# Attention scores copied to SBUF by the maximum pass, and one softmax scaling moved to the output copy

## What is computed

```python
def diff_core(q, k, v, lam):                       # "differential": 4 heads, two maps each
    s = einsum('bqhid,bkhid->bhiqk', q, k) * (DA ** -0.5)
    p = softmax(s, axis=-1)
    w = p[:, :, 0] - lam * p[:, :, 1]
    return einsum('bhqk,bkhd->bqhd', w, v)

def mla_core(qn, qr, kn, kr, v):                   # "latent": 8 heads
    s = (einsum('bqhd,bkhd->bhqk', qn, kn) + einsum('bqhd,bkd->bhqk', qr, kr)) * MLA_SCALE
    return einsum('bhqk,bkhd->bqhd', softmax(s, axis=-1), v)
```

## Time and profile before

| | us |
|---|---|
| median of 3 runs (4333.61 to 4336.67) | 4334.28 |
| the profiled execution | 4333.03 |
| its span in the trace | 4330.8 |
| PE busy | 3899.8 (90%) |
| VectorE busy | 2267.4 (52%) |
| ScalarE busy | 1575.8 (36%) |
| maxima L1061, x160 | 128.7 |
| exponentials from PSUM, 128x768, x128 | 113.8 |

### The profile page before, as it was taken

One profiled execution on the slowest core, in us unless ns is written; L12 is line 12 of the kernel. 1 busy time (PEld: TensorE's weight loads), 2 busy tenths in 40 slices (PEclk: granted clock), 3 DMA queues, 4 the chain that ended last, 5 costly groups with the idle time before them and its releaser, 6 DMA issues. The chain is left out here.

```text
span 4330.8 us, 53542 instructions
## 1 busy us (share of the span) xinstructions
PE 3899.8 (90%) x19922; PEld 3032.5 (70%) x19922; DVE 2267.4 (52%) x3759; ACT 1575.8 (36%) x2699; POOL 317.8 (7%) x282
## 2 busy tenths in 40 slices
PE   4987888999899898988899899979879998988998
PEld 3865556777788787865666588857568886657886
DVE  6345476854554475355632455354655535565552
ACT  2234463112443354234531344234444424343431
POOL 0000001111000000010000100002110010401001
PEclk8999999999999999999999999989889999989999
DMA  5100003552233244210012233322123322202332
GB/s 170 59 27 11 8 1 133 189 188 97 78 97 102 91 156 137 68 32 18 1 52 87 80 92 96 99 68 69 44 59 97 101 98 80 83 15 78 97 100 79
DMA packets 86727, 350.82 MB, mean 81 GB/s; under 512 B 9520, under 2 KB 9648, under 8 KB 85680
## 3 DMA queue, kind: packets, MB, share of 16 engines
q1 hardware_dynamic: 72752, 298.53, 21.9%
q0 software_dynamic: 13824, 50.34, 3.5%
HBM read 346.73 MB, written 2.10 MB: 81 GB/s over the span
## 5 line engine op out<-in xcount | busy, mean ns | idle before, releaser
L492 DVE TENSOR_TENSOR split_low<-weight_ring,split_high 128x1024 fp32r<-128x1024 f32 (+1 forms) x456 | 606.3, 1330 | 892.3 <-ACT split_high L484 877.5
L484 ACT ACTIVATE split_high<-weight_ring 128x1024 fp32r<-128x1024 f32 (+1 forms) x474 | 524.7, 1109 | 1043.6 <-PE banks L1364 470.0
L1492 PE MATMUL banks<-normed_high,split_high 128*128 128x512 f32 (+1 forms) x1760 | 654.0, 372 | 78.1 <-DVE normed_low L431 37.9
L1492 PE MATMUL banks<-normed_low,split_high 128*128 128x512 f32 (+1 forms) x1760 | 650.9, 370 | 0.0
L1492 PE MATMUL banks<-normed_high,split_low 128*128 128x512 f32 (+1 forms) x1760 | 650.6, 370 | 0.0
L1492 PEld LDWEIGHTS banks<-normed_high,split_high 128*128 128x128 f32 x1760 | 334.5, 190 | 141.2 <-issue 85.4
L1492 PEld LDWEIGHTS banks<-normed_low,split_high 128*128 128x128 f32 x1760 | 334.8, 190 | 55.0
L1492 PEld LDWEIGHTS banks<-normed_high,split_low 128*128 128x128 f32 x1760 | 334.3, 190 | 55.7
L1364 PE MATMUL banks<-hidden_high,split_high 128*128 128x512 f32 (+1 forms) x880 | 324.3, 369 | 8.0 <-DVE split_low L492 8.0
L1364 PE MATMUL banks<-hidden_low,split_high 128*128 128x512 f32 (+1 forms) x880 | 323.7, 368 | 0.0
L1364 PE MATMUL banks<-hidden_high,split_low 128*128 128x512 f32 (+1 forms) x880 | 323.7, 368 | 0.0
(11 more groups left out here) (286 smaller groups left out, 6757.7 us busy)
## 6 DMA issues: line engine op xcount, KB each, us to landing
weight_ring<-in_up SPq DMA_DIRECT2D x220, 512.0 KB, 3.6
weight_ring<-in_down SPq DMA_DIRECT2D x80, 704.0 KB, 4.0
modulation_ring<-in_ada POOLq DMA_DIRECT2D x80, 512.0 KB, 4.8
weight_ring<-in_merge SPq DMA_DIRECT2D x48, 768.0 KB, 4.5
weight_ring<-in_inputs SPq DMA_DIRECT2D x36, 512.0 KB, 3.6
weight_ring<-in_out SPq DMA_DIRECT2D x32, 512.0 KB, 3.6
latents<-in_ada POOLq DMA_DIRECT2D x16, 512.0 KB, 4.7
weight_ring<-in_xbc SPq DMA_DIRECT2D x16, 512.0 KB, 3.6
```

What stands on the lines that cost most here:

```text
L484: act.activation(k.splits[0][:, (n0 + panel) % RING, 0:width], k.slot(n0 + panel)[:, 0:width], ACT.Copy).then_inc(k.high_ready.sem, 1)
L492: dve.tensor_tensor(k.splits[1][:, s, 0:width], k.ring[:, s, 0:width], k.splits[0][:, s, 0:width].bitcast(F32), ALU.subtract).then_inc(k.l ...
L1492: last = pe.matmul(sums(r, half), w, x, start=(c + j == 0), stop=(c == KT - 1 and j == 2))
```

## The change

A column of zeros is written once. Differential and latent steps get it as their mask, repeated over all keys, so that they take the branches for masked steps: the maximum pass adds zero and writes the scores to `probs`, the exponential works there in place, and `scores_free` gives the maximum's semaphore. In differential steps map 0 isn't scaled any more: map 1's inverse is multiplied by map 0's sum besides -lambda, and the store multiplies the 128x128 output with map 0's inverse. Each reciprocal of such a step from t = 2 on also waits for the store before it. The parameter `adjacent`, true in all calls, goes away; the loops are those it had chosen.

```diff
@@ prepare @@
             dve.memset(k.head_squares[:, :], 1.0)
+            dve.memset(k.scalars[:, 14:15], 0.0)
...
@@ attention, VectorE, normalise @@
+                if combined and t >= 2:
+                    dve.wait_ge(*k.output_stored(t - 1))
                 link(dve.reciprocal(inverse, total))
                 if combined and j == 1:
-                    link(dve.tensor_tensor(inverse, inverse, step["subtract"], ALU.mult))
+                    link(dve.scalar_tensor_tensor(inverse, inverse, one(sums, m - 1), step["subtract"], ALU.mult,
+                                                  ALU.mult))
                     first = k.probs[:, (m - 1) % 4, 0:step["keys"]]
                     dve.scalar_tensor_tensor(first, p, inverse, first, ALU.mult, ALU.add).then_inc(
                         k.probs_ready.sem, 1)
                 elif combined:
-                    link(dve.tensor_scalar(p, p, inverse, None, ALU.mult))
+                    pass
...
@@ attention, VectorE, store @@
                     dve.wait_ge(*k.output_ready(t + 1))
-                    dve.tensor_copy(steps[t]["out"], result(t)).then_inc(k.output_stored.sem, 1)
+                    if combined:
+                        copied = dve.tensor_scalar(steps[t]["out"], result(t), one(inverses, 2 * t), None, ALU.mult)
+                    else:
+                        copied = dve.tensor_copy(steps[t]["out"], result(t))
+                    copied.then_inc(k.output_stored.sem, 1)
...
@@ mix_branches, differential @@
             steps.append(step(maps, end, [[values[:, c, P * h:P * h + P] for c in range(end // P)]],
-                              mixed[:, h, at:at + P], subtract=k.scalars[:, 8 + l:9 + l],
+                              mixed[:, h, at:at + P], mask=k.scalars[:, 14:15].to_broadcast([P, end]),
+                              subtract=k.scalars[:, 8 + l:9 + l],
                               square=squares[:, 6 * h + at // P:6 * h + at // P + 1]))
...
@@ mix_branches, latent @@
             steps.append(step(maps, end, [[values[:, c, 128 * pair + 64 * j:128 * pair + 64 * j + 64]
                                            for c in range(end // P)] for j in range(2)],
-                              mixed[:, 4 + pair, at:at + P]))
+                              mixed[:, 4 + pair, at:at + P], mask=k.scalars[:, 14:15].to_broadcast([P, end])))
```

More of the change, by code:

```diff
@@ L951, in project_latents, with attention @@
            constants_loaded=16)
-def attention(k, steps, turned, adjacent=False, scratch=None):
+def attention(k, steps, turned, scratch=None):
     nc = k.nc
@@ L988, in _, with score @@
         def _(pe):
-            def score(t, maps):
-                for j in maps:
+            def score(t):
+                for j in range(2):
                     if t >= 1:
@@ L1027, in _ @@
                 if t < U:
-                    score(t, (0, 1) if adjacent else (0,))
-                if not adjacent and t >= 2:
-                    weigh(t - 2)
+                    score(t)
                 if 1 <= t <= U:
                     turn(t - 1, 0)
-                if adjacent and t >= 2:
+                if t >= 2:
                     weigh(t - 2)
-                if not adjacent and t < U:
-                    score(t, (1,))
                 if 1 <= t <= U and per == 2:
@@ L1097, in _ @@
                     normalise(t - 1, 0)
-                    if adjacent:
-                        normalise(t - 1, 1)
+                    normalise(t - 1, 1)
                 if t < U:
                     maximum(t, 0)
[L1102 to L1105, removed]
+                    maximum(t, 1)
                 if t >= 2:
                     store(t - 2)
-                if t < U and not adjacent:
-                    maximum(t, 1)
             k.linked = linked
@@ L1144, in _ @@
             for t in range(U + 1):
-                if adjacent and 1 <= t:
+                if t >= 1:
                     copy(t - 1, 0)
@@ L1148, in _ @@
                     exponential(t, 0)
[L1149 to L1152, removed]
+                    exponential(t, 1)
                 if t >= 1 and per == 2:
                     copy(t - 1, 1)
-                if t < U:
-                    if not adjacent:
-                        exponential(t, 1)
                 if scratch is not None and t >= 3:
@@ L1671, in mix_branches @@
             steps.append(step(maps, end, [[values[:, c, P * h:P * h + P] for c in range(end // P)]],
-                              mixed[:, h, at:at + P], subtract=k.scalars[:, 8 + l:9 + l],
+                              mixed[:, h, at:at + P], mask=k.scalars[:, 14:15].to_broadcast([P, end]),
+                              subtract=k.scalars[:, 8 + l:9 + l],
                               square=squares[:, 6 * h + at // P:6 * h + at // P + 1]))
-    attention(k, steps, turned, adjacent=True, scratch=rope_queries.rearrange("p a b -> p (a b)").rearrange("p (a b) -> p a b", b=P))
+    attention(k, steps, turned, scratch=rope_queries.rearrange("p a b -> p (a b)").rearrange("p (a b) -> p a b", b=P))
     project_latents(k, l, context, mixed, keys, values, latents, rope_queries, squares)
@@ L1687, in mix_branches @@
                                            for c in range(end // P)] for j in range(2)],
-                              mixed[:, 4 + pair, at:at + P]))
-    attention(k, steps, turned, adjacent=True)
+                              mixed[:, 4 + pair, at:at + P], mask=k.scalars[:, 14:15].to_broadcast([P, end])))
+    attention(k, steps, turned)
     steps, wide = [], k.tables[:, 0:5 * P]
@@ L2198, in second_branches @@
                                   mask=k.table("wide")[:, BANK - end:BANK], gate=gate[1 + j], first=False, last=(j == 1)))
-    attention(k, steps, [tile[:, 24 + s, :] for s in range(4)], adjacent=True)
+    attention(k, steps, [tile[:, 24 + s, :] for s in range(4)])
 def plain_norm(k, gain, target, split=None, summed=True, ahead=0, block=None):
```

## The result

The changed kernel takes 4298.57 us (median of 4 runs, 4292.65 to 4299.79) against 4333.94 us before (4 runs, 4333.07 to 4336.67): ratio 0.9915, interval 0.9904 to 0.9927. A second set on another chip gave 4301.54 us (5 runs, 4293.32 to 4303.37) against 4330.53 (15 runs): 0.9932, interval 0.9919 to 0.9946. The forecast was 4312.5 us with a range from 4303 to 4322, a ratio of 0.995. The direction was right, and the gain was 35 us (29 in the second set) where 21.8 had been worked out.

The account below looks back on a forecast made before the run. TensorE nearly bounds latent steps; a loop of exponentials, combination, turn and copy bounds differential ones. Gains less losses made 21.7 us off the profiled 4333.0, plus 1.25 to reach the median's scale: 4312.5 us, range 4303 to 4322.

Parts of the forecast that it names:

- Latent, steady steps: Latent attention, 768-key steps: score released by the maximum, 6.61 to about 6.05 us, 24 x 0.56 = 13.4 us gained.
- Latent, from 256 to 768 keys: Latent attention, three steps reaching 768 keys from 256: TensorE goes earlier, 3 x 0.96 = 2.9 us gained.
- Stage starts: First scores of the stages start sooner: 1.8 and 1.2 us gained in latent attention, 2.7 in both differential stages.
- Differential attention, low clock: Layer 0's differential stage: three low-clock steps each shorten by 0.76 us through the early score, 2.3 us gained.
- 256-key steps: Differential attention, 8 steps of 256 keys: scaling no longer behind VectorE's late store, 0.2 us each, 1.6 us gained.
- Rival A: Layer 0's differential stage: the clock stays up, 4 to 8 us more gained, 4306 us; chance 0.13.
- Losses in the differential loop: Differential attention, 40 steps: exponentials from SBUF lose 2.2 us, the reciprocals' extra wait 2.0 us.
- added wait: Differential loop: reciprocals also wait for the store, 0.05 us a step, 40 x 0.05 = 2.0 us lost.
- C: Copying maximum becomes the bound: at 1.9 us a pass, differential loses 42 us, latent 7, 4383 us; chance 0.03.
- B: Latent attention: 24 steps become TensorE-bound and the clock nods to 0.95, gain 14 us, 4320 us; chance 0.12.
- D: Differential loss is larger, 8 us instead of 4.2, and the low clock gives nothing back: 4319 us; chance 0.05.
- Exponentials from SBUF by the page: Differential exponentials: the skill's page gives 43 ns more each, the rows 26; loss 3.4 us instead of 2.2.

Follow-up runs that it names:

- start kernels: Changed kernel with the first three steps of each differential and latent stage released late, 4308.05 us; with only those steps released early, 4326.68 us.
- differential attention alone: Changed kernel with latent attention put back as before, so only differential attention is changed: 4321.05 us against 4329.86, ratio 0.9979.
- filler kernel: Kernel before, with TensorE carrying out the weighing of each 256-key differential step three times, no wait changed: 4325.66 us against 4329.73, ratio 0.9992.

## Why the prediction missed

- **Latent, steady steps: right.** 6.61 to 6.05 us, from the sum of PE's parts. So were the price of the exponential (927 ns for 924) and the cover of the maxima.
- **Latent, from 256 to 768 keys: nearly right.** 6.09 to 5.07, 1.02 us for 0.96. Missed was the step behind it, 6.61 to 5.62 for 6.05: its weighing still belongs to 256 keys (0.66 us for 1.53), and TensorE waits 0.41 us before its second turn. 3 x 0.43 = 1.3 us.
- **Stage starts: sized from one profile.** 5.7 us were forecast. Between the first profiles it is far more, layer 1's latent start alone (first score to fourth) going from 15.60 + 10.02 = 25.62 us to 16.75, but the second profile of the same kernel has 22.35 there. The start kernels gave 6.5 to 9.6 us by their medians. A start is also not an end: in layer 1's differential stage the first four steps went from 24.4 to 19.8 us in the second profile, and the stretch behind the last score from 11.2 to 14.5, so that the stage lost 0.7 us. This term was not far off by those medians and can't be known closer than about 5 us in one execution.
- **Differential attention, low clock: the failed step.** The forecast said of a step at low clock that it "can go down to what PE is busy, 0.76 less; there are three such steps: 2.3 us". It took the low clock as given, in three steps, and priced only the wait under it. The runs show that the falls go away: layer 0's stage lost 11.2 us in both profiles of the changed kernel, where the sum had 2.75 for it (1.35 for the start, 2.3, 1.6 for 256-key steps, less 24 x 0.104), and differential attention alone lost 8.8 us in the median for 2.4. Behind the third step of the stage (from 294.00 us in the earlier trace rows's trace) the kernel before takes 107.82 us at a granted clock of 0.89, the filler kernel 100.04 and the second profile of the changed one 100.11, both at 1.00: the 7.7 us there are the clock alone, where the sum had 1.4. The filler shows that TensorE's own row decides this, without any change of waits. 8.4 us of the 9.8 us between the typical profile (31.5 us off) and the sum (21.7) are in this stage, 6.3 behind the third step and 2.1 at the start. Rival A had named it, with 0.13 and 4 to 8 us; its 4306 us lies 4 to 7 above the medians. The forecast held against A that TensorE's idle time only moves. That is so (9.30 us in a head after the change, 7.39 with the filler), and the clock stays up all the same. Its remark that the falls aren't in latent attention doesn't hold either: the fourth head of layer 0 had a step of 8.01 us in place of 6.61, and layer 1's granted clock was 0.93.
- **Losses in the differential loop: right in sum, wrong in parts.** 0.10 us a step were forecast, 0.054 for the exponentials and 0.05 for the added wait; 0.05 was measured in the 768-key steps. With the release and the copy, but the old scaling, the step is 5.12, so the dearer exponentials are paid for by the turn, which no longer stands behind a score (0.06 us behind the combination for 0.12). The added wait shows no cost; the product, forecast at nothing, costs 0.06. The 256-key steps were to give 1.6 us and gave nothing in sum: a head's six steps take 27.30 us, and 27.24 in the old schedule at full clock (filler).
- **Rivals.** C (the maximum becomes the bound) is refuted, 954 ns. B (the clock nods in full latent steps) is not seen: 6.05 in every steady step of both profiles. D had the loss too large.
- **Exponentials from SBUF by the page.** The section on the TRN2 errata in "VectorE: DVE Perf Modes" of the Trainium skill has 224 fixed cycles for ScalarE from SBUF and 172 from PSUM, at 1.2 GHz. The estimate from it is 43 ns for the difference; the rows give 927 - 898 = 29. The measurement decides.

What stays open: by which part of TensorE's row the early release keeps the clock up. It does not take idle time away: the second head has 9.30 us of it after the change, more than the 30.36 - 22.01 = 8.35 before. Nor is it the longest pause. Before the change that is 2.07 us, ahead of the score at 311.00, just before a fall; in the changed kernel it is longer, and the clock stays at 1.00:

```profile
325.04 0.87 PE L1008 MATMUL banks<-ones_and_identity,probs 128*128 128x128 f32 x6 [2.33 <-DVE probs L1080]
```

Open too is why a latent stage starts at the high clock in some executions and at the low one in others of the same kernel. No experiment here changed the work ahead of a latent stage, so its part in this was not tried.

## What to carry to other kernels

Ask of a wait that leaves TensorE idle also what it does to TensorE's clock elsewhere: the low-clock rows of layer 0's differential stage were a cost of the schedule here, and should not have been carried over into the sum. When a release is moved earlier, look for the loop that remains; here it was worth more (50 us in the two differential stages) than the release itself. Ask whether the engine that is relieved bounds the step: the same edit cost 0.05 us a step in one schedule and gained 0.49 in the other.

## What was not expected of the hardware

- The maximum pass that also writes 128x768 fp32 to SBUF takes 954 ns, the reduction that writes one column 953.
- A product of three [128,1] operands took 0.22 us, one of two 0.16.
- Repeating matmuls in TensorE's idle time shortened the six steps of a head by 3.1 us (30.36 to 27.24), with a granted clock of 1.00 in place of 0.83.
